# Strassen's scheme for chunks 2 and 3 of the output projection, on one NeuronCore

## The chip, the core and the metric

The kernel runs on one NeuronCore of a Trainium2 chip. The metric is the device time of one execution in microseconds (us); below it is the median of three. The core has TensorE (PE, matrix products, with its weight loader as PEld), VectorE (DVE), ScalarE (ACT), GpSimd (POOL) and SyncE (SP, which here only issues transfers), an on-chip memory of 128 partitions (SBUF), and eight accumulation banks of 128 x 512 float32 (PSUM).

## The reference, cut to what matters

One layer of a block with two attention branches over 512 tokens, width 2048, then a residual, and a final RMSNorm:

```
u = rms_norm(h, norm_gain)
proj = u @ w_in                                        # 2048 -> 13392 columns
y_sb = (stick_breaking(q, k, v) * silu(z_sb)) @ w_branch_sb
y_sa = (indexed_sparse(q, k, v, ...) * silu(z_sa)) @ w_branch_sa
mixed = sigmoid(g_sb) * y_sb + sigmoid(g_sa) * y_sa    # 512 x 2048
h = h + mixed @ w_out                                  # 512 x 2048 by 2048 x 2048
out = rms_norm(h, final_norm_gain)
```

The change concerns `mixed @ w_out` alone, and there two quarters of its output columns.

## The kernel before, in words

**Precision.** Every float32 operand of a large product is split in two fp32r tiles: `hi`, a copy made by ScalarE, and `lo`, the operand minus `hi`, made by VectorE. A product of two operands is then three matmuls, hi·hi, hi·lo and lo·hi, into one bank (`mm3`, lines 1178 to 1180).

**Chunks and strips.** All projections run as 34 chunks of 512 output columns, numbered `c`. A chunk is eight strips; strip `s` brings 256 rows of weights (two k-tiles of 128) by 512 columns. For a strip SP loads 512 KB into `stage` (two buffers), ScalarE makes `w_hi` (line 410), VectorE makes `w_lo` (line 721), both in rings of four, and TensorE multiplies: two k-tiles, four row tiles of the output, three matmuls, so 24 matmuls of 512 columns a strip and 192 a chunk. ScalarE and VectorE work two strips ahead of TensorE. The next load waits for the `w_lo` that frees its stage buffer, and `w_hi` waits for the strip four back to be used. TensorE waits at the head of each strip for its `w_lo` (`strip_lo`).

**The chunks around the change.** Chunks 26 to 29 are the branch projections: the first four strips of each make y_sb in the banks `proj0..3`, the last four y_sa in `attn0..3`. VectorE multiplies them with the sigmoids (`mix_sb` line 1080, `mix_both` lines 1090 and 1095), ScalarE makes the hi tile of the result (line 667) and VectorE the lo tile (line 1098), both in place in `area_r`, where tile pair `t` is k-tile `t` of the mixed activations. Chunks 30 to 33 (`C_OUT` to `C_LAST`) are the output projection, with the mixed activations as weights-side operand and `w_out` strips as the moving one. After each of the first three, VectorE adds the residual (line 1123), ScalarE sums the squares (line 687) and VectorE multiplies with the final gain (line 1127). The last chunk takes its first three strips tile by tile and the rest row tile by row tile, so that the rows end one after the other; then each row tile is normalized and stored.

**What sets the order.** Each engine's program is written out by hand and runs strictly in order; semaphores join them. POOL loads the residual `hres` (4 MB) and the gain `fgain` (1 MB over 128 partitions) when the branch chunks are through (line 396, `strip_used` of chunk 29).

Three lines on which most depends: the hi tile on ScalarE, VectorE's wait for it ahead of the lo tile, and SP's wait ahead of the load of strip `s`:

```
A(w_hi[:, s % RING, :, :], stage[:, s % 2, :, :], ACT.Copy).then_inc(strip_hi, 1)
dve.wait_ge(strip_hi, c * NS + (s + 1))
sp.wait_ge(strip_lo, c * NS + (s - 1))
```

## Time and profile before

| | us |
|---|---|
| median of 3 runs | 1597.68 (1597.47 to 1597.71) |
| the profiled execution | 1597.08 |
| its span, first to last instruction | 1595.5 |
| TensorE busy | 1585.0 |
| VectorE busy | 821.9 |
| ScalarE busy | 572.5 |
| outside the span (1597.08 - 1595.5) | 1.6 |

The page of the profile gives, engine by engine, busy time and share of the span; then the chain of work that ended last. Matmuls overlap one another in the pipeline, so their busy time says less than the distance from one start to the next. Times in the rows below count from the start of the span. A row of a stretch gives its ends and length, the busy time of PE, PEld, DVE, ACT and POOL with the number of instructions, then the granted TensorE clock (1.00 is 2.4 GHz, 0.50 is 1.2 GHz), the share of the DMA engines' time, and GB/s. A row of a timeline gives start, length (one instruction, or several in a row with their count), and in brackets how long the engine had been idle and what ended that.

### The profile page before, as it was taken

The numbers are of one execution on the slowest core, as the hardware profiler recorded it, in microseconds if no ns is written. First come the engines' busy times: TensorE is split into PE (matmuls) and PEld (weight loads), VectorE is DVE, ScalarE is ACT, GpSimd is POOL, SyncE is SP. The second block draws the span as 40 slices with busy tenths as digits, with TensorE's granted clock in tenths as the row PEclk, the third lists the DMA queues.
The fourth block names the chain that finished last, engine by engine and source line by source line (L and its number), as shares of the span: only waits on it lengthen the run. The fifth ranks groups of instructions, "written<-read, shape, count | busy, mean of one in ns | idle before, by whom it ended". The sixth has DMA issues, their size and how long they took to land.

```text
span 1595.5 us, 19959 instructions
## 1 busy us (share of the span) xinstructions
PE 1585.0 (99%) x7138; PEld 1317.2 (83%) x7138; DVE 821.9 (52%) x1183; ACT 572.5 (36%) x851; POOL 15.8 (1%) x35
## 2 busy tenths in 40 slices
PE   9999999999999999999999999999999999999997
PEld 7788888888888888888888888888888888888886
DVE  6853678522126655556564546554545545434333
ACT  5542333222224444334453332343332533323232
POOL 0000000000000000000000000000000000000000
PEclk9999999999999999999999999999999999999999
DMA  7223323333333333333334334333433522253223
GB/s 225 82 79 93 93 80 93 106 92 85 100 105 96 111 108 110 111 106 104 106 117 132 109 102 113 98 116 110 115 91 122 181 101 92 96 204 121 98 100 118
DMA packets 97979, 176.39 MB, mean 111 GB/s; under 512 B 11264, under 2 KB 24080, under 8 KB 97296
## 3 DMA queue, kind: packets, MB, share of 16 engines
q1 hardware_dynamic: 93712, 160.60, 33.4%
q0 software_dynamic: 3040, 13.63, 2.3%
q10 hardware_dynamic: 1184, 1.58, 0.3%
q8 instruction: 28, 0.46, 0.1%
q14 instruction: 15, 0.12, 0.0%
HBM read 156.90 MB, written 8.39 MB: 104 GB/s over the span
## 4 chain that ended last, share of the span: by engine, by line
PE 97%; ACT 1%; DVE 1%; DMA 1%; issue 0%; SPq 0%; ACTq 0%; DVEq 0%
PE proj L1178 29%; PE proj L1179 29%; PE proj L1180 29%; PE attn L1179 3%; PE attn L1180 3%; PE attn L1178 3%; DMA xs<-in_x 1%; PE attn L1313 1%; PE attn L1312 1%; ACT junk L463 0%; ACT w_hi L410 0%; DVE w_lo L721 0%; DVE xs L764 0%; DVE area L764 0%; ACT u_hi L443 0%
## 5 line engine op out<-in xcount | busy, mean ns | idle before, releaser
L1178 PE MATMUL proj<-u_hi,w_hi 128*128 128x512 f32 x1536 | 600.5, 391 | 0.5 <-DVE u_lo L774 0.5
L1180 PE MATMUL proj<-u_hi,w_lo 128*128 128x512 f32 x1536 | 598.9, 390 | 0.0
L1179 PE MATMUL proj<-u_lo,w_hi 128*128 128x512 f32 x1536 | 598.8, 390 | 0.0
L721 DVE TENSOR_TENSOR w_lo<-stage,w_hi 128x1024 fp32r<-128x1024 f32 x266 | 323.5, 1222 | 458.7 <-ACT w_hi L410 457.2
L410 ACT ACTIVATE w_hi<-stage 128x1024 fp32r<-128x1024 f32 x266 | 280.1, 1056 | 430.9 <-PE proj L1180 302.2
L1178 PEld LDWEIGHTS proj<-u_hi,w_hi 128*128 128x128 f32 x1536 | 288.8, 188 | 60.2 <-issue 1.3
L1180 PEld LDWEIGHTS proj<-u_hi,w_lo 128*128 128x128 f32 x1536 | 288.5, 188 | 60.2
L1179 PEld LDWEIGHTS proj<-u_lo,w_hi 128*128 128x128 f32 x1536 | 288.8, 188 | 58.7
L1178 PE MATMUL proj<-w_hi,u_hi 128*128 128x512 f32 x256 | 99.9, 390 | 0.0
L1180 PE MATMUL proj<-w_hi,u_lo 128*128 128x512 f32 x256 | 99.8, 390 | 0.0
L1179 PE MATMUL proj<-w_lo,u_hi 128*128 128x512 f32 x256 | 99.8, 390 | 0.0
L426 ACT ACTIVATE area<-proj 128x512 f32 (+1 forms) x80 | 47.8, 598 | 137.5 <-PE proj L1180 137.5
L1179 PE MATMUL proj<-w_lo,area_r 128*128 128x512 f32 x216 | 84.2, 390 | 0.0
L1178 PE MATMUL proj<-w_hi,area_r 128*128 128x512 f32 x216 | 84.1, 390 | 0.0
L1180 PE MATMUL proj<-w_hi,area_r 128*128 128x512 f32 x216 | 84.1, 390 | 0.0
L1005 DVE TENSOR_TENSOR x_lo<-x_in,x_hi 128x1280 fp32r<-128x1280 f32 x16 | 23.9, 1493 | 112.9 <-ACT x_hi L597 112.9
L597 ACT ACTIVATE x_hi<-x_in 128x1280 fp32r<-128x1280 f32 x16 | 20.4, 1275 | 151.9 <-DMA x_in<-turned 151.9
L1179 PEld LDWEIGHTS proj<-w_lo,u_hi 128*128 128x128 f32 x256 | 48.1, 188 | 10.0
L1178 PEld LDWEIGHTS proj<-w_hi,u_hi 128*128 128x128 f32 x256 | 48.1, 188 | 9.9
L1180 PEld LDWEIGHTS proj<-w_hi,u_lo 128*128 128x128 f32 x256 | 48.1, 188 | 9.9
L954 DVE RECIPROCAL og<-og 128x512 f32<-128x512 f32 x16 | 53.6, 3353 | 0.6
L528 ACT ACTIVATE relu<-attn 128x256 f32<-128x256 f32 (+2 forms) x48 | 21.0, 489 | 89.9 <-PE attn L1313 89.9
(175 smaller groups left out, 1413.0 us busy)
## 6 DMA issues: line engine op xcount, KB each, us to landing
stage<-in_w_in SPq DMA_DIRECT2D x208, 512.0 KB, 3.7
stage<-in_w_out SPq DMA_DIRECT2D x32, 512.0 KB, 3.6
x_in<-turned SPq DMA_DIRECT2D x256, 40.0 KB, 1.9
stage<-in_w_branch_sb SPq DMA_DIRECT2D x16, 512.0 KB, 3.6
stage<-in_w_branch_sa SPq DMA_DIRECT2D x16, 512.0 KB, 4.1
xs<-in_x SPq DMA_DIRECT2D x8, 512.0 KB, 8.0
o_scratch<-og POOLq DMA_DIRECT2D x16, 256.0 KB, 2.3
hres<-in_x POOLq DMA_DIRECT2D x1, 4096.0 KB, 13.6
```

Source lines behind the costliest of these rows:

```text
L410: A(w_hi[:, s % RING, :, :], stage[:, s % 2, :, :], ACT.Copy).then_inc(strip_hi, 1)
L426: A(dst(e), proj[e][:, :], ACT.Copy).then_inc(proj_free, 1)
L528: A(relu[:, n % 2, 0:WQ[qi]], attn[h % 4][:, 0:WQ[qi]], ACT.Relu).then_inc(relu_ready, 1)
L597: A(x_hi[:, :, :, :], x_in[:, :, :, :], ACT.Copy).then_inc(pt_hi, 1)
L721: V.tensor_tensor(w_lo[:, s % RING, :, :], stage[:, s % 2, :, :], w_hi[:, s % RING, :, :].bitcast(F), ALU.subtract).then_inc(strip_lo, 1)
L954: V.reciprocal(og[:, :], og[:, :]).then_inc(silu_step, 1)
L1005: V.tensor_tensor(x_lo[:, :, :, :], x_in[:, :, :, :], x_hi[:, :, :, :].bitcast(F), ALU.subtract).then_inc(w_low, 1)
L1178: nc.tensor.matmul(out_, a_hi, b_hi, start=start, stop=False, skip_group_check=free)
L1179: nc.tensor.matmul(out_, a_hi, b_lo, start=False, stop=False, skip_group_check=free)
L1180: return nc.tensor.matmul(out_, a_lo, b_hi, start=False, stop=stop, skip_group_check=free)
L1312: nc.tensor.matmul(o_, q, kix_lo[:, 0:WQ[qi]], start=True, stop=False)
L1313: nc.tensor.matmul(o_, q, kix_hi[:, 0:WQ[qi]], start=False, stop=True).then_inc(dots_done, 1)
```

## The change

Chunks 31 and 32 (columns 512 to 1535 of the output) are no longer computed as 192 matmuls each. Each is a product of 512 x 2048 activations and 2048 x 512 weights, taken as 2 x 2 blocks: tokens in two halves, k-tiles in even and odd ones, columns in two halves. Seven block products in the place of eight (the variant with 15 additions) give the result:

- of the activations, four combined tiles `e` for each pair of k-tiles, made once ahead of the two chunks (`e_build`, 4 VectorE instructions; `e_high` on ScalarE; `e_low` on VectorE), while chunks 29 and 30 run;
- of the weights, seven forms of 256 columns for each strip: three blocks as loaded and four sums (`form_sums`, 3 VectorE instructions), then one `form_high` on ScalarE and one `form_low` on VectorE over all seven;
- on TensorE `form_strip`: seven products x two row tiles x three matmuls = 42 matmuls of 256 columns for each of 16 strips, into seven of the eight banks;
- behind each chunk the seven products are joined with the residual (`blocks`, 11 VectorE instructions; the first product is copied out by ScalarE).

Chunk 33 keeps its 192 matmuls; its weights have a place of their own (`last_raw`), its banks are others, and its order in the programs of SP, ScalarE and VectorE is another. The products with the final gain of all three earlier chunks (`times_gain`) now stand behind everything of the two fast chunks. The residual is loaded in two parts, 3 MB when all mixed activations are there, and 1 MB late. Chunk 29 of ScalarE and VectorE stands outside its loop, chunk 30 as well.

```diff
+            def e_build(p):
+                def f():
+                    if p < 3:
+                        dve.wait_ge(strip_used, NS * (C_OUT - 1) + NS // 2)
+                    else:
+                        dve.wait_ge(strip_used, NS * C_OUT)
+                    dve.wait_ge(mix_lo, 2 * p + 2)
+                    if p:
+                        dve.wait_ge(e_part, 4 * p)
+                    V.tensor_tensor(a_raw[:, :, :].rearrange("p (k h) s -> p k (h s)", k=2),
+                                    area_r[:, 4 * p:4 * p + 3:2, :].bitcast(F),
+                                    area_r[:, 4 * p + 1:4 * p + 4:2, :].bitcast(F), ALU.add).then_inc(e_part, 1)
+                    dve.wait_ge(e_part, 4 * p + 1)
+                    V.tensor_tensor(e_raw[:, p, E7:E5 + 1, :], a_raw[:, 0:2, :], a_raw[:, 1:4:2, :],
+                                    ALU.subtract).then_inc(e_part, 1)
+                    dve.wait_ge(e_part, 4 * p + 2)
+                    V.tensor_tensor(e_raw[:, p, E6, :], e_raw[:, p, E5, :], a_raw[:, 0, :],
+                                    ALU.subtract).then_inc(e_part, 1)
+                    dve.wait_ge(e_part, 4 * p + 3)
+                    V.tensor_tensor(e_raw[:, p, E3, :], a_raw[:, 2, :], e_raw[:, p, E6, :], ALU.add).then_inc(e_part, 1)
+                return f
+            def e_low(p):
+                dve.wait_ge(e_hi_ready, p + 1)
+                V.tensor_tensor(e_lo[:, p, :, :], e_raw[:, p, :, :], e_hi[:, p, :, :].bitcast(F),
+                                ALU.subtract).then_inc(e_lo_ready, 1)
...
+            def e_next(p):
+                def f():
+                    e_build(p)()
+                    e_low(p - 1)
+                return f
+            chunk(C_OUT - 1, [None, None, None, None, e_build(0), mix_sb(C_OUT - 1), e_next(1), e_next(2)])
+            mix_both(C_OUT - 1)
...
+            def form_sums(q):
+                r = q % RAWS
+                dve.wait_ge(form_loaded[r], 64 * (q // RAWS + 1))
+                V.tensor_tensor(raw[r][:, S1:S3 + 1, :], raw[r][:, S1:S3 + 1, :], raw[r][:, B11:B22 + 1, :],
+                                ALU.add).then_inc(form_sum, 1)
+                dve.wait_ge(form_sum, 3 * q + 1)
+                V.tensor_tensor(raw[r][:, S2, :], raw[r][:, S3, :], raw[r][:, B11, :], ALU.add).then_inc(form_sum, 1)
+                dve.wait_ge(form_sum, 3 * q + 2)
+                V.tensor_tensor(raw[r][:, S4, :], raw[r][:, S2, :], raw[r][:, B21, :], ALU.add).then_inc(form_sum, 1)
+            def form_low(q):
+                dve.wait_ge(form_hi_ready, q + 1)
+                V.tensor_tensor(form_lo[q % RAWS][:, :, :], raw[q % RAWS][:, :, :],
+                                form_hi[q % HIS][:, :, :].bitcast(F), ALU.subtract).then_inc(form_lo_ready, 1)
...
-            for c in range(C_OUT, C_LAST):
...
-                residual(c)
...
+            for s in range(LEAD, NS):
+                split_lo(C_OUT, s)
+                if s == 2:
+                    e_low(2)
+                else:
+                    e_build(s)()
+                    if s > 3:
+                        e_low(s - 1)
+            form_sums(0)
+            form_sums(1)
+            e_low(7)
+            form_low(0)
...
+            for i in range(QT):
+                t = hres[:, i, 0:CW]
+                bank_done(dve, C_OUT, i)
+                V.tensor_tensor(t, proj[i][:, :], t, ALU.add).then_inc(h_ready, 1)
+            for q in range(FAST):
+                if q + 2 < FAST:
+                    form_sums(q + 2)
+                if q + 1 < FAST:
+                    form_low(q + 1)
+                if q == 7:
+                    blocks(0, 0, 8)
+                if q == 8:
+                    blocks(0, 8, BLOCK_STEPS)
+                if q == 15:
+                    blocks(1, 0, BLOCK_STEPS)
+                if q >= 12:
+                    last_low(q - 12)
+            for s in range(4, NS):
+                last_low(s)
+            times_gain(0)
+            times_gain(1)
+            times_gain(2)
```

ScalarE, then SP's loads of the forms and POOL, then TensorE:

```diff
+            def e_high(p):
+                def f():
+                    act.wait_ge(e_part, 4 * p + 4)
+                    A(e_hi[:, p, :, :], e_raw[:, p, :, :], ACT.Copy).then_inc(e_hi_ready, 1)
+                return f
...
+            chunk(C_OUT - 1, sigmoid_steps(C_OUT - 1) + [e_high(0), None, e_high(1), e_high(2)])
+            mix_high(C_OUT - 1)
...
+            for s in range(LEAD, NS):
+                split_hi(C_OUT, s)
+                if s >= 3:
+                    e_high(s)()
+            for q in range(FAST):
+                form_high(q)
...
+                if q == 8:
+                    first_product(0)
...
+            def load_forms(q):
+                if q < 2:
+                    sp.wait_ge(strip_used, NS * C_OUT + 6)
+                elif q < RAWS:
+                    sp.wait_ge(strip_used, NS * C_OUT + NS)
+                else:
+                    sp.wait_ge(form_used, q - RAWS + 1)
+                k, r = 2 * (q % NS), q % RAWS
+                for kt, part, form, copies in ((k, 1, B11, 1), (k + 1, 0, B22, 1), (k + 1, 1, B21, 1), (k, 0, S1, 2)):
+                    sp.dma_start(raw[r][:, form:form + copies, :],
+                                 wout[:, kt:kt + 1, out_cols(q, part)].to_broadcast([P, copies, HW])
+                                 ).then_inc(form_loaded[r], 16)
+            def load_last(s):
+                sp.wait_ge(form_used, NS + s + 1)
+                sp.dma_start(last_raw[:, 2 * s:2 * s + 2, :],
+                             wout[:, 2 * s:2 * s + 2, CW * 3:D_MODEL]).then_inc(last_loaded[s], 16)
...
-            pool.wait_ge(strip_used, NS * C_OUT)
-            pool.dma_start(hres[:, :, :], x[0].rearrange("(i p) d -> p i d", p=P)).then_inc(res_loaded, 16)
+            pool.wait_ge(mix_lo, KT)
+            pool.dma_start(hres[:, :, :], x[0].rearrange("(i p) d -> p i d", p=P)[:, :, 0:3 * CW]).then_inc(res_loaded, 16)
...
+            pool.wait_ge(form_used, FAST - 2)
+            pool.dma_start(hres_last[:, :, :], x[0].rearrange("(i p) d -> p i d", p=P)[:, :, 3 * CW:D_MODEL]
+                           ).then_inc(last_res, 16)
...
+            def form_strip(q):
+                m, s = q // NS, q % NS
+                k0, k1 = 4 * s, 4 * s + 2
+                pe.wait_ge(form_lo_ready, q + 1)
+                if m == 0:
+                    pe.wait_ge(e_lo_ready, s + 1)
...
+                for p, (left, form) in enumerate(products):
+                    if s == 0:
+                        product_free(m, p)
+                    for t in range(2):
+                        a_hi, a_lo = left(t)
+                        i = mm3(product_bank(m, p)[:, HW * t:HW * t + HW], a_hi, a_lo,
+                                form_hi[q % HIS][:, form, :], form_lo[q % RAWS][:, form, :],
+                                s == 0 and t == 0, s == NS - 1, True)
```

The order of the instructions shows what VectorE has between the last mixed activations and the end of chunk 30. Before, in the order of the program (`area_r` is the last lo tile of the activations, `w_lo` a strip's lo tile, `hres<-proj` the residual of chunk 30):

```order
L1095 TENSOR_TENSOR mix<-mix,mix_sa 128x512
L1098 TENSOR_TENSOR area_r<-mix,area_r 128x512 x4
L1113 REGISTER_ALU
L1113 COMPARE_AND_BRANCH
L721 TENSOR_TENSOR w_lo<-stage,w_hi 128x1024 x8
L1123 TENSOR_TENSOR hres<-proj,hres 128x512 x4
L1127 TENSOR_TENSOR hres<-hres,fgain 128x512 x4
```

And now, from the same place on, to the second build in chunk 30:

```order
L1211 TENSOR_TENSOR area_r<-mix,area_r 128x512 x4
L834 TENSOR_TENSOR w_lo_60<-stage_62,w_hi_56 128x1024
L1250 TENSOR_TENSOR e_lo<-e_raw,e_hi 128x1024
L834 TENSOR_TENSOR w_lo_61<-stage_63,w_hi_57 128x1024
L1235 TENSOR_TENSOR a_raw<-area_r 128x1024
L1239 TENSOR_TENSOR e_raw<-a_raw 128x512
L1242 TENSOR_TENSOR e_raw<-e_raw,a_raw 128x256
L1245 TENSOR_TENSOR e_raw<-a_raw,e_raw 128x256
L834 TENSOR_TENSOR w_lo_58<-stage_62,w_hi_54 128x1024
L1235 TENSOR_TENSOR a_raw<-area_r 128x1024
```

Between two `w_lo` stand four instructions of a build and, from the next on, an `e_lo`. ScalarE at the same place had nothing but `w_hi`; now an `e_hi`, which needs the build, stands ahead of the next `w_hi`:

```order
L741 ACTIVATE area_r<-mix 128x512 x4
L484 ACTIVATE w_hi_56<-stage_62 128x1024
L484 ACTIVATE w_hi_57<-stage_63 128x1024
L752 ACTIVATE e_hi<-e_raw 128x1024
L484 ACTIVATE w_hi_54<-stage_62 128x1024
L752 ACTIVATE e_hi<-e_raw 128x1024
L484 ACTIVATE w_hi_55<-stage_63 128x1024
```

The third place is VectorE where the first fast chunk ends and the second begins, from `form_low(8)` to `form_low(9)` (`L1319` are steps of `blocks`):

```order
L1277 TENSOR_TENSOR form_lo_99<-raw_95,form_hi_105 128x1792
L1319 TENSOR_TENSOR hres<-hres,t_sum 128x2x256
L1319 TENSOR_TENSOR t_sum<-attn,t_sum 128x512
L1319 TENSOR_TENSOR u_sum<-attn,t_sum 128x512
L1319 TENSOR_TENSOR hres<-attn,hres 128x2x256
L1319 TENSOR_TENSOR hres<-proj,hres 128x2x256 x3
L1319 TENSOR_TENSOR hres<-hres,u_sum 128x2x256
L1268 TENSOR_TENSOR raw_97<-raw_97 128x512
L1271 TENSOR_TENSOR raw_97<-raw_97 128x256
L1273 TENSOR_TENSOR raw_97<-raw_97 128x256
L1277 TENSOR_TENSOR form_lo_100<-raw_96,form_hi_103 128x1792
```

Eight steps of `blocks` stand ahead of what strip 9 needs; before, VectorE had one `w_lo` between two strips there.

## Rows read from the trace of the kernel before

**Rows 1.** The page: span, and the chain that ended last by engine

```profile
span 1595.5 us, 19959 instructions
...
PE 97%; ACT 1%; DVE 1%; DMA 1%; issue 0%; SPq 0%; ACTq 0%; DVEq 0%
```

**Rows 2.** Stretches of chunks 30, 32: length, busy per engine, clock, DMA

```profile
1413.10:1456.70 43.60, 43.60 (x194) 36.11 (x194) 16.56 (x19) 11.70 (x16) 1.28 (x2) 1.00 0.58 217
...
1500.20:1543.70 43.50, 43.50 (x193) 36.08 (x192) 15.84 (x17) 12.09 (x18) 0.00 (x0) 1.00 0.31 107
```

**Rows 3.** Timeline, PE, 256 then 128 columns: start, us, operation

```profile
521.50 0.29 PE L1178 MATMUL attn<-x_hi,vh 128*128 128x256 f32 x1
521.62 0.28 PE L1179 MATMUL attn<-x_lo,vh 128*128 128x256 f32 x1
521.74 0.28 PE L1180 MATMUL attn<-x_hi,vl 128*128 128x256 f32 x1
521.86 0.23 PE L1178 MATMUL attn<-x_hi,vh 128*128 128x128 f32 x1
521.92 0.28 PE L1179 MATMUL attn<-x_lo,vh 128*128 128x128 f32 x1
522.03 0.28 PE L1180 MATMUL attn<-x_hi,vl 128*128 128x128 f32 x1
```

**Rows 4.** Groups by line and shape: busy us, mean ns, idle before

```profile
L721 DVE TENSOR_TENSOR w_lo<-stage,w_hi 128x1024 fp32r<-128x1024 f32 x266 | 323.5, 1222 | 458.7 <-ACT w_hi L410 457.2
...
L979 DVE TENSOR_TENSOR p_sa<-attn,p_sa 128x256 f32<-128x256 f32 x8 | 3.4, 425 | 0.3
...
L1005 DVE TENSOR_TENSOR x_lo<-x_in,x_hi 128x1280 fp32r<-128x1280 f32 x16 | 23.9, 1493 | 112.9 <-ACT x_hi L597 112.9
...
L410 ACT ACTIVATE w_hi<-stage 128x1024 fp32r<-128x1024 f32 x266 | 280.1, 1056 | 430.9 <-PE proj L1180 302.2
```

**Rows 5.** Timeline of DVE in chunks 29 and 30

```profile
1393.84 2.48 DVE L1080 TENSOR_TENSOR mix<-proj,area 128x512 f32<-128x512 f32 x4
...
1409.40 0.69 DVE L1090 TENSOR_TENSOR mix_sa<-attn,area 128x512 f32<-128x512 f32 x1 [4.60 <-PE attn L1180]
1410.23 0.69 DVE L1095 TENSOR_TENSOR mix<-mix,mix_sa 128x512 f32<-128x512 f32 x1
1411.14 0.69 DVE L1090 TENSOR_TENSOR mix_sa<-attn,area 128x512 f32<-128x512 f32 x1 [0.22 <-DVE mix L1095]
1411.87 0.69 DVE L1095 TENSOR_TENSOR mix<-mix,mix_sa 128x512 f32<-128x512 f32 x1
...
1418.17 2.35 DVE L721 TENSOR_TENSOR w_lo<-stage,w_hi 128x1024 fp32r<-128x1024 f32 x2
1431.90 1.23 DVE L721 TENSOR_TENSOR w_lo<-stage,w_hi 128x1024 fp32r<-128x1024 f32 x1 [11.38 <-ACT w_hi L410]
```

**Rows 6.** Timeline of ACT in chunk 30

```profile
1430.81 1.06 ACT L410 ACTIVATE w_hi<-stage 128x1024 fp32r<-128x1024 f32 x1 [12.26 <-DMA stage<-in_w_out]
```

**Rows 7.** Transfers of chunk 30: ns of issue, us to landing, GB/s

```profile
L292 SPq DMA_DIRECT2D stage<-in_w_out x9: 372/373/373, 1405.0 to 1448.5; - x9
...
DMA to landing us min/median/max: 3.5/3.6/12.3
...
hres<-in_x POOLq DMA_DIRECT2D x1, 4096.0 KB, 13.6
...
1418.00:1423.00 5.00, 5.00 (x24) 4.14 (x23) 2.52 (x3) 0.55 (x1) 0.00 (x0) 1.00 1.01 428
```

**Rows 8.** Transfers on the page: 128 KB, us to landing

```profile
out_h<-hres ACTq DMA_DIRECT2D x4, 128.0 KB, 2.0
```

**Rows 9.** Last matmul, and the clock in stretches after it

```profile
1587.01 0.39 PE L1180 MATMUL proj<-last_hi,area_r 128*128 128x512 f32 x1
...
1591.00:1592.00 1.00, 0.00 (x0) 0.00 (x0) 0.32 (x1) 0.43 (x1) 0.00 (x0) 1.00 0.26 89
1592.00:1593.00 1.00, 0.00 (x0) 0.00 (x0) 0.00 (x0) 0.00 (x0) 0.00 (x0) 0.70 1.07 401
```

More of the change, by code:

```diff
@@ L86, in build @@
     region("area", 32 * TILE)
-    region("stage", 2 * 2 * TILE)
-    region("w_hi", RING * 2 * TILE)
-    region("w_lo", RING * 2 * TILE)
+    region("small", SMALL)
+    STRIP = 2 * TILE
+    ring = region("ring", (2 + 2 * RING) * STRIP)
     work = region("work", 11 * TILE + 2 * 4 * TRI)
-    region("small", SMALL)
     region("far", 4 * TRI)
```

278 lines of the change are left out of this document (195 added, 83 removed).

## The prediction, made before the change was run

> **What bounds the kernel now.** I read the chain of waits first: 97% of it is TensorE, over a span of 1595.5 us [rows 1]. Then the stretches. In each of the five chunks from 29 on TensorE is busy for the whole 43.5 us and takes 192 matmuls; chunks 30 and 32 stand for them [rows 2]. So a chunk is 43.5 us, a strip of 24 matmuls 5.44 us, a matmul of 512 columns 0.227 us, and the engine that feeds it never lets it wait. VectorE is busy for 16.6 us in chunk 30 and 15.8 us in chunk 32 [rows 2]; the rest is waiting for its turn. Chunk 30 begins at 1413.1 and ends at 1456.7 [rows 2].
>
> **TensorE's gain.** 16 strips of 42 matmuls are 672 of 256 columns, where 384 of 512 were: 7/8 of the columns. What a matmul of 256 columns costs stands in a V product: starts at 521.50, 521.62, 521.74, 521.86, so 0.12 us each [rows 3]. With 128 columns the next starts come after 0.06, 0.11 and so on: 0.11 us is what a new stationary tile costs at least [rows 3]. I take 0.12: a form strip is 42 x 0.12 = 5.04 us, both chunks are 80.6 us where 87.0 were, a gain of 6.4 us. The lower end is 0.11, 73.9 us.
>
> The Trainium skill ("TensorE: Matmul & The Clock Gate", section Back-to-back issue gap) gives columns / 2.4 GHz + 2.5 ns, 109 ns for 256; the trace disagrees (120 ns for 256, 227 where that rule gives 216). By that rule the gain would be 13.7 us in the place of 6.4.
>
> **What VectorE must do for it.** Its prices: 1024 elements 1.22 us, 1280 1.49, 256 0.42 [rows 4], 512 0.69 [rows 5]. 256 elements more cost 0.27, so `form_low` over 1792 takes about 2.03 us. Two instructions in a row overlap: two of 1024 take 2.35 [rows 5], so the queue moves on after about 1.15. One that waits for the one before starts 0.04 us after its end (1411.14 + 0.69 to 1411.87), with a second wait 0.14 to 0.22 (1409.40 to 1410.23, 1410.23 to 1411.14) [rows 5]. So an `e_build` is 1.22 + 0.69 + 0.42 + 0.42, three steps of 0.04 and some 0.2 ahead: 3.1 us. `form_sums` is 1.55 (0.69 + 0.42 + 0.42 + 0.08, less the overlap), and a step of `blocks` 0.73 or, with a second wait, 0.83. A form strip needs 1.55 + 2.0 = 3.55 us of VectorE for 5.04 us of TensorE. That is room, as long as nothing else stands between.
>
> **Chunk 29.** `e_build(0)` waits until four strips are used (1391.4). From there, in order: build 3.1; `e_hi` (1.06) and the next `w_hi` (1.06) on ScalarE, since `e_hi` now stands ahead of it, 2.2 with the signals; `w_lo` 1.2; `mix_sb` 2.5 [rows 5]; `w_lo` 1.2; build 3.0; 2.2; `w_lo` 1.2; build 3.0; `e_low` 1.1. That is 20.7 us, to 1412.1, where `mix_both` began at 1409.40. It takes until 1418.17 before [rows 5], so until 1420.8 now. TensorE needs nothing of this before 1424, so it costs nothing by itself.
>
> **Chunk 30.** VectorE: `w_lo`, `e_lo`, `w_lo`, 3.5 us, to 1424.3, build(3) to 1427.3. The load of strip 4 is issued after the first of these, at 1422.0. Usually a strip lands after 3.6 us, but here one took 12.3 [rows 7], and ScalarE sat 12.26 us until 1430.81 for it [rows 6]: the residual and the gain, 5.2 MB, filled the DMA engines at 428 GB/s (the residual landed after 13.6 us) [rows 7]. The change starts them at 1420.8 and not at 1413.1, and they are 4.2 MB: 9.8 us at that rate plus some 2 of start, so to about 1432.5. I let strip 4 land at 1432.0, 10 us after issue; the ends are 3.6 and 12.3. Then `w_hi` and `w_lo` end at 1434.3; TensorE wants them at 1413.1 + 4 x 5.44 = 1434.9.
>
> From here a ring decides: `w_lo(s)`, `e_build(s)`, `e_high(s)`, `w_hi(s+1)`, `w_lo(s+1)`, each waiting for the one before, 3.1 + 2.2 + 1.15 = 6.4 us a strip against TensorE's 5.44. So the `w_lo` end at 1440.7, 1447.1 and 1453.5 (wanted: 1440.3, 1445.7, 1451.2). Chunk 30 ends 2.3 us late, at 1459.0. Behind its last `w_lo` VectorE has build(7), `e_low(6)`, two `form_sums`, `e_low(7)`, `form_low(0)`: 3.1 + 1.1 + 3.1 + 1.2 + 2.0 = 10.5, to 1464.0. TensorE waits for that: **7.3 us** later than 1456.7, 5.0 of them idle in one piece. If strip 4 landed at once, the builds alone would still hold `w_lo(4)` until 1427.3 + 2.2 + 1.2 = 1430.7 (3.7 us late in all); with 12.3 us it is 9.6.
>
> **Fast chunks.** Ahead of `form_low(1)` stand four residuals (2.8), and `form_sums(2)` (1.55): 2.8 + 1.55 + 2.0 = 6.35 against 5.04, **1.3 us** late. Then it runs level: the four loads of a form strip start when the strip four back is used; SP takes 0.37 us to issue one [rows 7], and a 128 KB transfer lands after 2.0 us [rows 8], so 3.6 to 4.5, I take 4.1. No transfer of 256-column rows from the weights is in the trace, and 3.6 to 12.3 are a strip's bounds [rows 7]; above 6.5 (two strips, 10.1, less 3.55) every second strip would be late by the rest. At the seam strip 9 is late: from the start of strip 6, load 4.1, sums 1.55, `form_low(8)` 2.0, eight steps 6.6, sums 1.55, `form_low(9)` 2.0 = 17.8 against 3 x 5.04: **2.7 us**. Strip 10: three steps 2.3 + 1.55 + 2.0 = 5.85 against 5.04: **0.8**. The banks of the second chunk come free 0.3 to 2 us ahead of use. From strip 12 `last_low` is added: 3.55 + 1.15 = 4.7, still under 5.04. At the second seam the 11 steps (9.2 us) lie beside 16.3 us of strips of the last chunk which are ready, the 12 gain products (7.4) too. The last chunk keeps its 43.5 us and the tail stays.
>
> **The sum.** 1597.1 (the profiled execution: span 1595.5, 1.6 around it) - 6.4 + 7.3 + 1.3 + 2.7 + 0.8 = 1602.8. The median lies 0.6 above the profiled execution: **1603.4 us**. With both ends of strip 4's landing 1599.8 to 1605.7.
>
> **Rivals.** All further times on the median's scale.
>
> (1) *The feed is hidden.* VectorE's pure work from 1420.8 to `form_low(0)` is 6 `w_lo`, 5 builds, 6 `e_lo`, 3.1 and 2.0: 35 us, ready at 1456, just when TensorE arrives. Its waits for ScalarE and the DMA (8 us) make the delay; if they fall away (the last `e_hi` and `w_hi` overlapping more than I see, strip 4 landing early), the 7.3 are gone: 1596.1, no slower than before. It decides at `w_lo(4)`: ended by 1427, all is hidden. For it: the work fits. Against: the strict order on ScalarE, and 12.26 us of wait in the row.
>
> (2) *256 columns cost 0.11.* Gain 13.1; but strips of 4.62 us meet the same VectorE: 7.3, 6.35 - 4.62 = 1.7, 17.8 - 13.9 = 3.9, 5.85 - 4.62 = 1.2 and, from strip 12, 4 x 0.08 = 0.3 make 14.4: 1599.0. Against: four starts in a row at 0.12. With (1) as well 1591.7.
>
> (3) *The clock falls.* After the last matmul (start 1587.01, length 0.39) the clock was 1.00 up to 1592 and 0.70 in the mean of the next us [rows 9]: it fell some 5 us after, and my idle piece has 5.0. A strip at 1.2 GHz takes 5 us more, of which the late strip 1 hides 1.3; one strip at that level makes 1607.
>
> The Trainium skill ("TensorE: Matmul & The Clock Gate", section The HAM clock gate) has the same two levels, with the lower one after idleness; the trace agrees, with the fall behind the last matmul.
>
> (4) *Loads of the forms land late*, at 7.0 us rather than 4.1: the seam grows by 2.9, and every second strip is 0.5 late, six times: 1609.3.
>
> **Chances.** My walk 0.50 (1600 to 1606.5); clock or late loads 0.18; hidden feed 0.19; 0.11 us matmuls alone 0.08; both 0.05. What a measurement of this kernel can tell from no change is about 0.2%, 3.2 us. Faster by more: only with both, 0.05, and a rest of (1) 0.02: 0.07. Within: the rest of (1), (2), and of my walk what lies under 1600.9, 0.07: 0.32. Slower: 0.61. The range runs from 1595.5, which leaves out the cases with both, to 1609.5.
>
> **What would show it.** After: starts of the 256-column matmuls 0.12 apart. `w_lo` of strips 4 to 7 of chunk 30 6.4 us apart. The first form matmul near 1464, having waited for `form_lo`. The second form strip 1.3, the tenth 2.7, the eleventh 0.8 us late, otherwise 5.04. ScalarE waiting for strip 4's DMA until about 1432. The clock at 1.00 throughout. I am wrong if TensorE starts the forms before 1459, or if the pitch in the strips is under 0.115.

## The result: 0.44% slower, and the profile after

| | before | after |
|---|---|---|
| median | 1597.71 us | 1604.69 us |
| lowest to highest | 1597.47 to 1598.13 (5 runs) | 1603.47 to 1605.72 (5 runs) |
| profiled execution, its span | 1597.08, 1595.5 us | 1603.47, 1601.8 us |
| ratio, 95% interval | | 1.0044, 1.0033 to 1.0055 |

The forecast was 1603.4 us, with a range of 1595.5 to 1609.5. The page of the changed kernel has the same two lines as [rows 1]: the span, and the chain that ended last.

```profile
span 1601.8 us, 20545 instructions
...
PE 92%; DVE 4%; ACT 1%; issue 1%; DMA 1%; DVEq 0%; ACTq 0%
```

TensorE's share of the chain fell from 97% to 92%, and VectorE's rose from 1% to 4%: the engine that was always busy now waits for the one that feeds it. How often, and on what, the list of waits between 1450 and 1560 us says (engine, line and tile that waited, whom for, total us, times, longest):

```profile
PE attn L1393 <- DVE form_lo L1277: 4.3, 1, 4.3
...
PE proj L1393 <- DVE form_lo L1277: 3.1, 1, 3.1
```

Two large idle pieces, then, and both end with `form_lo`: at the entry to the form chunks and at the seam between them. TensorE's timeline shows the places (start, length, operation, idle time ahead and who ended it):

```profile
1458.52 0.39 PE L1395 MATMUL proj<-w_hi,area_r 128*128 128x512 f32 x1
1463.17 0.58 PE L1393 MATMUL attn<-form_hi,area_r 128*128 128x256 f32 x1 [4.27 <-DVE form_lo L1277]
1463.55 0.42 PE L1394 MATMUL attn<-form_lo,area_r 128*128 128x256 f32 x1
1463.77 0.42 PE L1395 MATMUL attn<-form_hi,area_r 128*128 128x256 f32 x1
1463.98 0.41 PE L1393 MATMUL attn<-form_hi,area_r 128*128 128x256 f32 x1
...
1509.70 0.28 PE L1394 MATMUL proj<-form_lo,e_hi 128*128 128x256 f32 x1
1509.82 0.28 PE L1395 MATMUL proj<-form_hi,e_lo 128*128 128x256 f32 x1
1513.18 0.39 PE L1393 MATMUL proj<-form_hi,area_r 128*128 128x256 f32 x1 [3.08 <-DVE form_lo L1277]
```

At 1509 the starts are 0.12 us apart, as in [rows 3]. At 1463 the same matmul takes 0.21 us. The stretches say why (bounds, length, busy us and instructions of PE, PEld, DVE, ACT and POOL, then the granted clock, DMA share, GB/s):

```profile
1413.10:1459.10 46.00, 44.79 (x194) 35.65 (x192) 34.52 (x45) 13.88 (x16) 1.29 (x2) 1.00 0.47 166
...
1463.00:1463.50 0.50, 0.33 (x1) 0.33 (x2) 0.50 (x2) 0.00 (x0) 0.00 (x0) 0.50 0.85 295
...
1469.83:1474.87 5.04, 5.04 (x44) 5.04 (x43) 3.04 (x4) 4.08 (x8) 0.00 (x0) 1.00 0.44 130
...
1514.00:1516.00 2.00, 2.00 (x12) 2.00 (x11) 1.86 (x4) 0.00 (x0) 0.00 (x0) 0.50 0.88 284
```

The first row answers to chunk 30 in [rows 2]: TensorE was busy for 44.8 us where it was for 43.6, its last matmul of the chunk started at 1458.52 and not at 1456.45, and VectorE was busy for 34.5 us where it was for 16.6. The third is a stretch as long as one form strip, from 0.2 us into strip 1 on, at full clock and with no gap: 5.04 us. The second and the fourth show the granted clock at 0.50, 1.2 GHz. It stayed there for 3.4 us each time: at the entry from 0.4 us before the end of the idle piece on, at the seam from 0.8 us after its end.

VectorE's timeline, for the feed and the entry (compare [rows 5]), then the seam:

```profile
1433.63 1.23 DVE L834 TENSOR_TENSOR w_lo<-stage,w_hi 128x1024 fp32r<-128x1024 f32 x1 [7.77 <-ACT w_hi L484]
...
1439.71 1.22 DVE L834 TENSOR_TENSOR w_lo<-stage,w_hi 128x1024 fp32r<-128x1024 f32 x1 [0.94 <-ACT w_hi L484]
...
1461.10 2.02 DVE L1277 TENSOR_TENSOR form_lo<-raw,form_hi 128x1792 fp32r<-128x1792 f32 x1
1463.04 2.48 DVE L1338 TENSOR_TENSOR hres<-proj,hres 128x512 f32<-128x512 f32 x4
...
1503.55 0.69 DVE L1319 TENSOR_TENSOR hres<-hres,t_sum 128x512 f32<-128x512 f32 x1
...
1509.59 0.68 DVE L1268 TENSOR_TENSOR raw<-raw 128x512 f32<-128x512 f32 x1
...
1511.11 2.02 DVE L1277 TENSOR_TENSOR form_lo<-raw,form_hi 128x1792 fp32r<-128x1792 f32 x1
```

And ScalarE in chunk 30 (compare [rows 6]), with the strip's load:

```profile
1432.54 1.06 ACT L484 ACTIVATE w_hi<-stage 128x1024 fp32r<-128x1024 f32 x1 [5.58 <-DMA stage<-in_w_out]
1437.67 1.06 ACT L752 ACTIVATE e_hi<-e_raw 128x1024 fp32r<-128x1024 f32 x1 [4.07 <-DVE e_raw L1245]
1438.63 1.04 ACT L484 ACTIVATE w_hi<-stage 128x1024 fp32r<-128x1024 f32 x1
```

The last two rows and VectorE's second are the ring of the prediction: `e_hi` waits for the build, the next `w_hi` stands behind it, the next `w_lo` waits for that. The whole difference of the two spans, by TensorE's starts in its timeline:

| place | measured | predicted |
|---|---|---|
| 672 matmuls of 256 columns at 0.120 us | -6.4 us | -6.4 |
| first form matmul at 1463.17, not 1456.68 | +6.5 | +7.3 |
| form strip 0 takes 6.45 us, not 5.04 | +1.4 (clock) | +1.3 (late `form_lo`) |
| form strip 8 takes 8.28 | +3.2 | +2.7 |
| form strip 9 takes 6.62 | +1.6 (clock) | +0.8 (late `form_lo`) |
| the other 12 that can be timed this way | 0 | 0 |
| sum | +6.3, as the spans differ | +5.7 |

### The profile page after: what moved, and what is told of

Read it like the earlier page. It is cut to its first block, busy times and chain, and to the rows that moved or that the text cites. A ratio compares the mean times of both kernels' runs of the same rounds, so it can differ in the third digit from the quotient of the medians.

```text
span 1601.8 us, 20545 instructions
## 1 busy us (share of the span) xinstructions
PE 1582.9 (99%) x7426; PEld 1327.0 (83%) x7426; DVE 896.8 (56%) x1285; ACT 591.7 (37%) x861; POOL 16.5 (1%) x36
## 4 chain that ended last, share of the span: by engine, by line
PE 92%; DVE 4%; ACT 1%; issue 1%; DMA 1%; DVEq 0%; ACTq 0%
PE proj L1393 26%; PE proj L1394 26%; PE proj L1395 26%; PE attn L1394 5%; PE attn L1395 4%; PE attn L1393 4%; DMA stage<-in_w_out 1%; ACT w_hi L484 1%; DVE a_raw L1235 1%; PE attn L1526 1%; PE attn L1525 1%; ACT junk L537 0%; DVE w_lo L834 0%; DVE e_raw L1239 0%; DVE form_lo L1277 0%
## 5 line engine op out<-in xcount | busy, mean ns | idle before, releaser
L834 DVE TENSOR_TENSOR w_lo<-stage,w_hi 128x1024 fp32r<-128x1024 f32 x247 | 300.4, 1222 | 392.8 <-ACT w_hi L484 391.2
L484 ACT ACTIVATE w_hi<-stage 128x1024 fp32r<-128x1024 f32 x247 | 260.0, 1055 | 348.7 <-PE proj L1395 246.9
L1395 PEld LDWEIGHTS proj<-w_hi,u_lo 128*128 128x128 f32 x256 | 48.0, 188 | 10.1
L1008 DVE SCALAR_TENSOR_TENSOR score<-relu,wix,score 128x256 f32<-128x256 f32 (+2 forms) x45 | 27.8, 618 | 47.0 <-ACT relu L602 44.5
L1393 PE MATMUL attn<-u_hi,w_hi 128*128 128x512 f32 x128 | 49.8, 389 | 0.0
L1394 PE MATMUL attn<-u_lo,w_hi 128*128 128x512 f32 x128 | 49.8, 389 | 0.0
```

Source lines behind the costliest of these rows:

```text
L484: A(w_hi[s % RING][:, :, :], stage[s % 2][:, :, :], ACT.Copy).then_inc(strip_hi, 1)
L834: V.tensor_tensor(w_lo[s % RING][:, :, :], stage[s % 2][:, :, :], w_hi[s % RING][:, :, :].bitcast(F), ALU.subtract).then_inc(strip_lo, 1)
L1008: V.scalar_tensor_tensor(acc, relu[:, n % 2, 0:w], wix[:, qi, h:h + 1], acc, ALU.mult, ALU.add).then_inc(relu_used, 1)
L1393: nc.tensor.matmul(out_, a_hi, b_hi, start=start, stop=False, skip_group_check=free)
L1394: nc.tensor.matmul(out_, a_hi, b_lo, start=False, stop=False, skip_group_check=free)
L1395: return nc.tensor.matmul(out_, a_lo, b_hi, start=False, stop=stop, skip_group_check=free)
```

## The experiments

Eleven kernels were run. The kernel before ran beside them, with medians of 1597.2 to 1597.6; "after" is 1604.7 and was not run again. Each bracket gives the lowest and highest time, then the ratio to the kernel before and its 95% interval. The starts of strips below are those of TensorE's first matmul of each.

**The ring on ScalarE.** The split of the next strip goes ahead of the A form of this one; nothing else is changed.

```diff
             for s in range(LEAD, NS):
                 split_hi(C_OUT, s)
-                if s >= 3:
-                    e_high(s)()
+                if s >= 4:
+                    e_high(s - 1)()
+            e_high(7)()
```

> One edit to the changed kernel: in chunk 30 ScalarE makes the hi tile of weight strip s ahead of the e_hi of pair s-1, so that the ring w_lo, build, e_hi, w_hi, w_lo is open. Everything is computed. Theory (the ring and VectorE's queue set when the first form strip starts): w_lo of strips 5 to 7 no longer wait 0.94 us each, chunk 30 ends on time near 1456.8, the first form matmul starts at about 1460.3 in the place of 1463.4, the idle piece shrinks to 3.5 us, and the median is 3 to 4.5 us under the changed kernel's 1604.7, about 1600.8. Rival (the late landing of strip 4 alone sets it, and VectorE has room): the first form matmul stays within 1 us of 1463.4, and the median at 1604.

1600.53 us (1599.72 to 1602.82; against before 1.0021, 1.0011 to 1.0030). In the profiled run the last matmul of chunk 30 started at 1456.54 instead of 1458.52, so the chunk was on time, and the forms at 1460.07 instead of 1463.17. Strip 4 had come as late as ever:

```profile
1433.60 1.22 DVE L835 TENSOR_TENSOR w_lo<-stage,w_hi 128x1024 fp32r<-128x1024 f32 x1 [7.76 <-ACT w_hi L484]
...
1438.66 1.22 DVE L835 TENSOR_TENSOR w_lo<-stage,w_hi 128x1024 fp32r<-128x1024 f32 x1
```

The next `w_lo` now comes after 5.06 us instead of 6.08, faster than TensorE uses a strip (5.44). With the strips this close together chunk 30 catches up on the late strip 4. TensorE still stood for 3.5 us ahead of the forms, and the clock fell there; this profiled run (1602.82) is the slowest of the ten.

**The residual's load later.** POOL issues it only when strip 5 of chunk 30 is split, behind the loads of the strips.

```diff
             pool.wait_ge(mix_lo, KT)
+            pool.wait_ge(strip_lo, NS * C_OUT + 6)
...
```

> One edit to the changed kernel: POOL issues the loads of the residual and the gain only when the w_lo of strip 5 of chunk 30 is made, so that strips 4 and 5 do not share the DMA engines with them. Everything is computed. Theory (the loads of 4.2 MB hold strip 4 back, and the ring carries that to the end of the chunk): strip 4 lands some 3.7 us after issue, near 1424.5, its w_lo starts near 1428 in the place of 1433.6, all else in chunk 30 moves 5.5 us ahead, the first form matmul starts at about 1458, the clock does not fall there; median about 6 us under the changed kernel's, 1598.6. Rival (VectorE's own work sets it): w_lo of strip 4 moves but the first form strip does not start before 1462, and the median stays above 1603.

1600.32 us (1599.74 to 1604.75; 1.0019, 1.0010 to 1.0029). First the strips. These are the loads of strips from 1416 to 1434 us, of the changed kernel and then of this one: ns of issue, first and last start, and the time to landing.

```profile
L337 SPq DMA_DIRECT2D stage<-in_w_out x2: 368/368/368, 1420.8 to 1423.1; - x2
...
DMA to landing us min/median/max: 11.7/12.9/14.1
```

```profile
L337 SPq DMA_DIRECT2D stage<-in_w_out x3: 368/368/368, 1420.7 to 1429.1; - x3
...
DMA to landing us min/median/max: 3.5/3.6/4.0
```

So it was the residual's load that kept strip 4 away, as [rows 7] suggested. The order on ScalarE was the old one here, and the `w_lo` still came 6.08 us apart, but from 1427.80 on, 5.8 us earlier, and the last matmul of chunk 30 started at 1456.40: on time as well. So it takes both, the late strip 4 and the ring, to make chunk 30 late, and either edit alone takes that away. The forms started at 1458.49. But the gain fell short of what was expected, and the profiled run (1604.75, the slowest of the ten) shows a wait that I had not thought of:

```profile
1464.20 0.69 DVE L1269 TENSOR_TENSOR raw<-raw 128x512 f32<-128x512 f32 x1 [3.37 <-DMA raw<-in_w_out]
...
1465.72 2.02 DVE L1278 TENSOR_TENSOR form_lo<-raw,form_hi 128x1792 fp32r<-128x1792 f32 x1
```

The sums of strip 2 wait 3.4 us for their load, and `form_lo` of strip 1, whose operands are long there, stands behind them in VectorE's queue. TensorE stood 4.0 us for it until 1467.80. In the kernel after this wait was covered, since the forms began 4.7 us later. How much of it the other nine runs had is not known; the edit below that removes it took only 0.3 us more off the median.

**VectorE's order at the seam.** First form: `form_lo` of strips 8 and 9, seven block steps, sums and `form_lo` of 10, then the last four steps.

```diff
+                if q == 9:
+                    form_low(10)
+                    blocks(0, 7, BLOCK_STEPS)
                 if q + 2 < FAST:
                     form_sums(q + 2)
-                if q + 1 < FAST:
+                if q + 1 < FAST and q not in (8, 9):
                     form_low(q + 1)
                 if q == 7:
-                    blocks(0, 0, 8)
-                if q == 8:
-                    blocks(0, 8, BLOCK_STEPS)
+                    form_low(9)
+                if q == 7:
+                    blocks(0, 0, 7)
```

> One edit to the changed kernel, VectorE's order at the seam of the two fast chunks: form_low(9) right behind form_low(8), then seven steps of blocks, form_sums(10), form_low(10), and only then the last four steps. Everything is computed. Theory (strip 9 is late because eight steps of blocks stand ahead of its form_low): the wait of 3.1 us ahead of strip 9 goes; in its place the second chunk's seventh product waits for its bank about 1.2 us inside strip 8; the clock does not fall at the seam, so strip 10 is not 1.6 us longer; in all 3 to 3.6 us under the changed kernel's median, about 1601.3. Rival (the late loads of forms 9 and 10 set it): strip 9 stays at least 2 us late and the median within 1 us of 1604.7.

1604.70 us (1603.91 to 1605.85; 1.0048, 1.0031 to 1.0065): nothing gained, a miss. Strip 9 took 5.04 us behind a strip 8 of 6.43, but strip 10 took 7.61, for TensorE stood ahead of strip 11:

```profile
1525.17 0.39 PE L1396 MATMUL proj<-form_hi,area_r 128*128 128x256 f32 x1 [2.42 <-DVE form_lo L1277]
```

The lateness was handed on, not taken away. A second form, seven steps, then `form_lo` of strip 9 at once:

```diff
+                if q == 8:
+                    form_low(9)
                 if q + 2 < FAST:
                     form_sums(q + 2)
-                if q + 1 < FAST:
+                if q == 8:
+                    blocks(0, 7, 10)
+                if q == 9:
+                    blocks(0, 10, BLOCK_STEPS)
+                if q + 1 < FAST and q != 8:
                     form_low(q + 1)
                 if q == 7:
-                    blocks(0, 0, 8)
-                if q == 8:
-                    blocks(0, 8, BLOCK_STEPS)
+                    blocks(0, 0, 7)
```

> Only VectorE's order at the seam of the two chunks of forms is another: seven of the eleven block steps, then form_lo of strip 9, then the sums of strip 10 and the steps behind it. The last of the seven steps ended at about 1509.0 us in the trace of the changed kernel, so form_lo of strip 9 ends at 1511.0 and TensorE, which wants it at 1510.15, waits about 0.9 us instead of 3.24. Theory that the clock's fall at 1514 follows from that one idle piece: no fall, strip 9 takes 5.04 us instead of 6.62, and the time is 1604.7 - 2.4 - 1.6 = 1600.7. Rival: the fall comes whatever the idle piece: 1602.3. Strips 10 and 11 are to start on time in both; if they don't, the lateness has only moved, as in the first form of this experiment.

1603.14 us (1602.39 to 1604.24; 1.0036, 1.0022 to 1.0049). Strip 9 was 0.8 us late, about as worked out, but strip 10 then 2.6, and the clock fell after that. Theory and rival both had strips 10 and 11 on time; neither held.

**The clock at the entry.** 18 matmuls of 512 columns, whose results nothing reads, fill the idle piece ahead of the forms.

```diff
+            pe.wait_ge(attn_free, 4 * QT)
+            for _ in range(18):
+                nc.tensor.matmul(attn[0][:, :], area_r[:, 0, 0:P], area_r[:, 0, :], start=True, stop=True)
             for q in range(FAST):
                 form_strip(q)
```

> One edit to the changed kernel: ahead of the first form strip TensorE runs 18 matmuls of 512 columns (4.1 us) into a bank whose content is replaced afterwards, so that it is not idle for 4.65 us there. They are work beside the computation; everything is computed as before. Theory (the clock falls since TensorE is idle, but VectorE's form_low(1), ready at 1468.96, would have held strip 1 anyway): the clock stays at 1.00 there, the first form strip takes 5.04 us in the place of 6.45, strip 1 then waits until about 1469.0, so only 0.8 us are won: median about 1603.9. Rival (the fallen clock costs its full 1.4 us and VectorE is not late): 1603.3, and strip 1 starts 5.04 us behind strip 0 without a wait.

1602.61 us (1601.63 to 1604.97; 1.0036, 1.0023 to 1.0048). The stretches of the entry and of the seam:

```profile
1457.00:1463.00 6.00, 5.92 (x27) 4.56 (x25) 5.86 (x9) 3.29 (x2) 0.00 (x0) 1.00 0.40 113
1463.00:1467.00 4.00, 3.87 (x32) 3.87 (x33) 3.93 (x9) 0.00 (x0) 0.00 (x0) 1.00 0.47 159
1509.00:1513.00 4.00, 1.25 (x10) 1.05 (x9) 3.90 (x6) 1.70 (x1) 0.00 (x0) 1.00 0.52 132
1513.00:1517.00 4.00, 4.00 (x36) 4.00 (x35) 3.83 (x6) 1.07 (x1) 0.00 (x0) 1.00 0.52 166
```

With TensorE busy the clock stays at 1.00. What that gives is small, since VectorE's own lateness comes out from behind it: strip 1 was late by 0.8 us, so strip 0 took 5.85 where it had been 6.45, and strip 10 late by 0.5. The seam kept its clock too in this run, behind an idle piece of 3.0 us where 3.4 had cost it, and strip 9 took 5.57 instead of 6.62; neither expectation had that. With 0.3 us less in strip 8 these make the 1.8 us between the two profiled spans (1600.0 and 1601.8).

**The wait found in the second experiment.** The residual later as above, and `form_lo` of strip 1 ahead of the residual adds and of the sums of strip 2.

```diff
             form_low(0)
+            form_low(1)
             dve.wait_ge(res_loaded, 16)
...
-                if q + 1 < FAST:
+                if 0 < q and q + 1 < FAST:
```

> The residual's load waits for strip 5 of the chunk ahead (as in the run before), and form_lo of strip 1 is made ahead of the four residual adds and of the sums of strip 2. Theory: the idle piece of 4.3 us ahead of strip 1 was VectorE standing at the load of strip 2 with form_lo of strip 1 queued behind that wait; it goes, form_lo of strip 1 ends at about 1461, strip 1 starts 5.04 us behind strip 0, and the time is 1604.7 - 4.8 (forms start at 1458.6 instead of 1463.4) - 1.4 (no clock fall in strip 0) + 0.8 (strip 2 waits for its form_lo, about 1469.5) = 1599.3. Rival: the load itself is what is late, strip 2 then waits the 4 us that strip 1 waited: about 1602.

1600.03 us (1598.72 to 1603.30; 1.0019, 1.0010 to 1.0029). Strip 1 no longer waits, and strip 2 comes 5.04 us after it: the rival is out. The forms began at 1459.82, though, 1.2 us later than worked out, and the clock fell after an idle piece of 2.8 us, so strip 0 took 6.62.

**Entry and seam, first try.** The ring, the later residual, `form_lo` of strip 1 early and the second form of the seam.

> Four edits together: ScalarE splits a strip ahead of the A forms, the residual's load waits for strip 5, form_lo of strip 1 ahead of the residual adds, and form_lo of strip 9 behind seven block steps. If each lateness is its own and none is behind another: forms start at about 1457.7 (-5.7), no clock fall in strips 0 and 9 (-1.4 and -1.6), strip 9 late by 0.9 instead of 3.24 (-2.4), strip 2 late by 0.8: 1604.7 - 10.3 = 1594.4, below the kernel before at 1597.3. Rival: strips 2 and 3 take over the lateness of the entry, since their loads start only when the last strip of the chunk ahead is used: about 1598.

1597.41 us (1595.96 to 1600.60; 1.0002, 0.9993 to 1.0011): the loss is gone, but 3 us more than the first theory gives. The rival had its time nearly right and its cause wrong: strips 2 and 3 were on time to 0.1 us. The loss is again ahead of strip 10, with the clock behind it:

```profile
1512.19 0.39 PE L1400 MATMUL proj<-form_hi,area_r 128*128 128x256 f32 x1 [2.33 <-DVE form_lo L1279]
```

```profile
1513.00:1515.00 2.00, 2.00 (x13) 2.00 (x12) 1.97 (x3) 1.97 (x5) 0.00 (x0) 0.57 0.89 250
```

**`form_lo` always ahead of the next sums.** To let no `form_lo` stand behind a load, I turned the two around in every strip, moved `form_lo` of 10 and 11 forward at the seam, and ran that alone, then the entry alone, then both. The entry is the three edits above with one more: `e_lo` of strip 7 ahead of the first sums, where VectorE waits for the DMA. The seam:

```diff
-                if q + 2 < FAST:
-                    form_sums(q + 2)
-                if q + 1 < FAST:
+                if q + 1 < FAST and q != 9:
                     form_low(q + 1)
+                if q + 2 < FAST and q != 9:
+                    form_sums(q + 2)
                 if q == 7:
-                    blocks(0, 0, 8)
+                    blocks(0, 0, 7)
                 if q == 8:
-                    blocks(0, 8, BLOCK_STEPS)
+                    form_sums(11)
+                    form_low(10)
+                    blocks(0, 7, BLOCK_STEPS)
```

> Only VectorE's order: each form_lo ahead of the sums of the strip behind the next (so that it doesn't stand behind their load), and at the seam: seven block steps, form_lo of strip 9, sums of 10 and 11, form_lo of 10, the last four block steps, form_lo of 11. Theory: the two orders tried so far moved the lateness to strip 11 and to strip 10, because form_lo stood behind block steps there too while its form_hi was long made; with both moved, strips 9, 10 and 11 are on time within 0.3 us and the clock does not fall there: 1604.7 - 3.2 - 1.6 = 1599.9. Rival: VectorE has no room for eleven block steps within three strips at all, and about 2.5 us stay somewhere: 1602 to 1603.

1603.79 us (1603.45 to 1604.23; 1.0038, 1.0025 to 1.0052). A miss: strip 8 took 8.63 us and strip 9, with the clock, 6.62. The block steps began 6.3 us after TensorE began strip 7, where in the kernel after it was 3.7.

> Only the entry: ScalarE splits a strip ahead of the A forms, the residual's load waits for strip 5, e_lo of strip 7 goes into VectorE's idle time at the load of the forms instead of standing ahead of form_lo of strip 0, and form_lo of strip 1 ahead of the residual adds. Theory: form_lo of strip 0 then starts at about 1455.2 and ends at 1457.2, TensorE has some 0.8 us without work instead of 4.65, the clock does not fall in strip 0: 1604.7 - (1463.4 - 1457.2) - 1.4 = 1597.1. Rival: if the start of the forms is gained but the seam's lateness grows (loads there later), 1598.5.

1597.81 us (1596.77 to 1599.04; 1.0000, 0.9991 to 1.0009). The forms began at 1457.51 after 0.8 us without work, with the clock at 1.00; strip 2 was 1.0 us late. The entry gives 6.9 us of the 7.6 expected. In the profiled run (1599.04, the slowest of the ten) the seam had grown, as the rival said: strip 8 took 8.79 us and strip 9 7.52.

> Both edits together. If the entry and the seam cost on their own, the gains add: 1604.7 - 7.6 - 4.8 = 1592.3, faster than the kernel before (1597.2) by 0.3%; that is also the time that 672 matmuls at 0.120 us without any idle piece give against the old chunks (1597.7 - 6.4 + 0.8 = 1592.1). Rival: one lateness hides behind the other and the sum of gains is smaller: 1595.

1598.93 us (1598.02 to 1600.05; 1.0009, 1.0000 to 1.0018), a us above the entry alone. A reason stands in VectorE's timeline of this kernel, and in its list of waits from 1460 to 1560:

```profile
1492.71 2.03 DVE L1279 TENSOR_TENSOR form_lo<-raw,form_hi 128x1792 fp32r<-128x1792 f32 x1 [1.77 <-ACT form_hi L777]
...
1498.02 2.02 DVE L1279 TENSOR_TENSOR form_lo<-raw,form_hi 128x1792 fp32r<-128x1792 f32 x1 [1.77 <-ACT form_hi L777]
```

```profile
DVE form_lo L1279 <- ACT form_hi L777: 17.4, 12, 1.8
```

Sums, `form_hi` on ScalarE, `form_lo`: with `form_lo` next in the queue nothing lies beside the `form_hi` of the same strip, so VectorE stands for it, 1.77 us at the most, twelve times, 17.4 us in all. The loop takes 5.31 us (1492.71 to 1498.02), and TensorE's strips 3 to 7 came out at 5.31 to 5.32 instead of 5.04. The order that looked like a hazard, sums of the next but one strip first, is what hides ScalarE. It also brought VectorE late to the block steps, at 1501.48, 6.7 us after TensorE began strip 7, and strip 8 took 8.76 us.

**The old order in the steady strips, the new one at the seam only.**

```diff
-                if q + 2 < FAST:
+                if q + 2 < FAST and q not in (7, 8, 9, 10):
                     form_sums(q + 2)
-                if q + 1 < FAST:
+                if 0 < q and q + 1 < FAST and q != 9:
                     form_low(q + 1)
+                if q in (7, 8, 10):
+                    form_sums(q + 2)
                 if q == 7:
-                    blocks(0, 0, 8)
+                    blocks(0, 0, 7)
                 if q == 8:
-                    blocks(0, 8, BLOCK_STEPS)
+                    form_sums(11)
+                    form_low(10)
+                    blocks(0, 7, BLOCK_STEPS)
```

> As the run before (entry and seam), but the sums of the strip after the next stand ahead of form_lo again, as in the changed kernel, except at the seam. Theory: with form_lo first, VectorE's chain sums, form_hi, form_lo had nothing between its links, and came out at 5.31 us a strip against TensorE's 5.04; by strip 8 the block steps then started 2 us late. With the old order in the steady strips, form_lo of strip 8 ends at about 1494, the block steps start at 1495.5 and form_lo of strip 9 ends at 1503.1, before TensorE wants it: strips 9, 10 and 11 start on time, no clock fall, forms from 1457.6 with one piece of 1.1 us ahead of strip 2: 1604.7 - 5.8 - 1.4 + 1.1 - 3.2 - 1.6 = 1593.8, below the kernel before (1597.4) by 0.2%. Rival: the block steps themselves can't be hidden within three strips: about 1596.

**1592.81 us** (1592.17 to 1594.96, 10 runs), against the kernel before 0.9974, 0.9964 to 0.9983: faster than both. Its page, its waits of TensorE in the form chunks, and a stretch as long as four strips, from 0.3 us into strip 8 on:

```profile
span 1591.2 us, 20546 instructions
```

```profile
PE attn L1400 <- DVE form_lo L1279: 0.9, 1, 0.9
```

```profile
1499.32:1519.48 20.16, 20.16 (x171) 20.16 (x170) 18.11 (x24) 10.91 (x14) 0.00 (x0) 1.00 0.68 200
```

Four strips in 20.16 us, 4 x 5.04, with VectorE busy for 18.1 of them. Its timeline there shows how the steps fit:

```profile
1490.34 3.95 DVE L1279 TENSOR_TENSOR form_lo<-raw,form_hi 128x1792 fp32r<-128x1792 f32 x2
...
1495.78 0.68 DVE L1321 TENSOR_TENSOR hres<-hres,t_sum 128x512 f32<-128x512 f32 x1
...
1501.09 2.02 DVE L1279 TENSOR_TENSOR form_lo<-raw,form_hi 128x1792 fp32r<-128x1792 f32 x1
...
1506.40 2.02 DVE L1279 TENSOR_TENSOR form_lo<-raw,form_hi 128x1792 fp32r<-128x1792 f32 x1 [0.25 <-ACT form_hi L777]
...
1511.19 2.01 DVE L1279 TENSOR_TENSOR form_lo<-raw,form_hi 128x1792 fp32r<-128x1792 f32 x1
```

`form_lo` of strips 7 and 8 together while the load of strip 9 is on its way; the block steps begin at 1495.78, 1.8 us after TensorE began strip 7, so close behind its products; each later `form_lo` ends before TensorE wants it (1503.1 for 1504.1, 1508.4 for 1509.1, 1513.2 for 1514.2). Against the changed kernel's profiled run the span is 10.6 us shorter, and TensorE's starts place all of it: forms start 5.6 earlier, strip 0 is 1.3 shorter (clock), strips 1 and 2 are 1.1 longer (late `form_lo` of strip 2), strip 8 is 3.2 and strip 9 1.6 shorter.

## Why the prediction was right, step by step

- **The gain.** 0.120 us for a matmul of 256 columns, nearly everywhere at full clock; 5.04 us in 12 of the 15 strips whose successor gives their end. Right, and (2) of the rivals is out. By the formula of the Trainium skill ("TensorE: Matmul & The Clock Gate", section Back-to-back issue gap), which it gives for an isolated matmul, 109 ns, a strip would take 4.6 us; the trace disagrees, no strip of any run is under 5.04.
- **Chunk 29.** `mix_both` was put at 1412.1 and started at 1411.30, and the operands were done at 1419.7, not 1420.8. Right to a us; TensorE waited for nothing there.
- **Strip 4's load.** Put at 10 us to landing; 11.7 measured, issued at 1420.8 and not 1422.0, so its landing, 1432.5, was only 0.5 off. The second experiment takes the cause away and gets 3.5 to 4.0; it also shows that my lower end, 3.7 us late in all with an early landing, was too high: the forms started at 1458.49, 1.8 us late.
- **The ring.** 6.4 us a strip predicted, 6.08 measured, three times: a build took 2.9 us and not 3.1, and `e_hi` (1437.67) and `w_hi` (1438.63) overlap by 0.1. Chunk 30 ended 2.1 us late instead of 2.3. The first two experiments show that it needs both the order on ScalarE and the late strip 4.
- **The entry.** 1463.2 for 1464.0. Behind its last `w_lo` VectorE worked without a gap from 1453.0 to 1463.1, 10.1 us where I had 10.5.
- **Strips 1 and 10.** Here the sizes agree and the mechanism doesn't. I had 1.3 and 0.8 us of late `form_lo`. What was there is the clock at 1.2 GHz for 3.4 us at each idle piece: matmuls at 0.213 instead of 0.120, 1.4 and 1.6 us. `form_lo` was late beneath that and hidden by it; in the fourth experiment, with the clock at 1.00, it comes out as 0.8 and 0.5 us. That 2.1 us of the one came near 3.0 of the other is luck. Rival (3) held that the clock stays up unless it is idle for 5 us, and that a fall costs a whole strip, 5 us. Both its condition and its price were wrong. The condition I read from a single event in [rows 9]: that the clock is still 1.00 some time after a last matmul doesn't say that a shorter pause leaves it alone. The price took a whole strip at that level, which no row showed. "The clock at 1.00 throughout" was the one line of the check list that failed.
- **The seam.** 2.7 predicted, 3.24 measured. From the start of strip 6 (1494.82) to the end of `form_lo(9)` (1513.13) it took 18.3 us, where I had 17.8. Two errors stand against each other there: the load was in after 5.3 us and not 4.1 (the sums began at 1500.09), and the eight steps took 6.0 us (1503.55 to 1509.59) and not 6.6.
- **Loads of forms.** In the median a 128 KB load landed after 2.5 us and the 256 KB one, issued last of the four, after 3.8. VectorE waited for a strip's loads nine times, 15.6 us in all, and in these its sums began 4.7 to 6.2 us after the strip four back was through, where I had taken 4.1. That was too low, but it stays under the 6.5 from which strips would have been late, so rival (4) is out.
- **Rival (1).** Out in the kernel as changed (`w_lo` of strip 4 ended at 1434.9, not 1427). Its premise, that the work fits and the order makes the delay, is what the last experiment confirms: between the profiled spans 4.3 of the 6.4 us of gain are left (1591.2 against 1595.5), with 0.9 lost at the first form matmul (1457.54) and 1.2 in strips 0 to 2. The forecast of rival (1), 1596.1, lies above the 1592.8 because it let the 4.8 us of the later strips stand.

In the order of the table the measured terms differ from the predicted ones by -0.8, +0.1, +0.5 and +0.8. That this comes to only 0.6 us is partly luck. The forecast was 1.3 us too low; the rest of that is that the median lay 1.2 us above the profiled execution, where I had 0.6.

## What to carry to other kernels

A cheaper algorithm on the busiest engine pays only when its feed still fits in the shorter time, and fits in order: here VectorE's work was 18 of 20 us in the tightest stretch, and the same instructions in another order on two engines, with one load issued later, were worth 12 us, nearly twice the gain of the algorithm. Look for the queue in which a ready instruction stands behind a wait, and for the pair of instructions on two engines with nothing between them: both errors were made here, the second one in mending the first. And look strip by strip where the lateness went before judging a repair: alone, three orders for the seam showed 0 to 1.6 us, since what was late moved one or two strips on or stayed. The order that worked was run only together with the entry, so what it gives alone is not known.
